# Two layers of a hybrid recurrent decoder on one core: another order of the projections' steps, and the norm's statistics shared between ScalarE and VectorE

## What is computed

```python
for l in range(DEPTH):                       # 2 layers; x is (tokens, 1024)
    x = sublayer(x, 0, lambda h: _swiglu(h, wg0, wu0, wd0))
    x = sublayer(x, 1, mixers)               # p = h @ w_in; 3 head groups; y @ w_out
    x = sublayer(x, 2, lambda h: _swiglu(h, wg1, wu1, wd1))

def sublayer(x, i, f):                       # shift, scale, gate = c @ w_ada + b_ada
    y = f(x * (1 + scale[i]) + shift[i])
    return LN(ALPHA * x + w[i] * (1 + gate[i]) * y)     # mean and variance over 1024 features

def mixers(h):
    p = h @ w_in                             # RWKV-7 part | GLA part | mLSTM part
    kk = k * k_k; kk = kk * rsqrt(sum(kk * kk, per head))   # RWKV-7: "KK"
    ...                                      # chunked recurrences of the three groups
    return concat(y_rwkv, y_gla, y_mlstm) @ w_out
```

## Time and profile before

| | us |
|---|---|
| median of three runs | 1681.7 |
| lowest and highest of them | 1667.69, 1681.84 |
| the profiled execution | 1677.3 |
| span of its profile | 1675.5 |
| busy: PE, DVE, ACT, POOL | 1608.5, 936.3, 667.0, 203.6 |

### The profile page before, as it was taken

One profiled execution on the slowest core, in us unless ns is written; L12 is line 12 of the kernel. 1 busy time (PEld: TensorE's weight loads), 2 busy tenths in 40 slices (PEclk: granted clock), 3 DMA queues, 4 the chain that ended last, 5 costly groups with the idle time before them and its releaser, 6 DMA issues. The chain is left out here.

```text
span 1675.5 us, 32875 instructions
## 1 busy us (share of the span) xinstructions
PE 1608.5 (96%) x14052; PEld 1480.5 (88%) x14052; DVE 936.3 (56%) x1605; ACT 667.0 (40%) x985; POOL 203.6 (12%) x271
## 2 busy tenths in 40 slices
PE   5999999999999999999999999999999999999997
PEld 2999998998767789999989999989877768899996
DVE  1544545586653775555474544466946456655544
ACT  2333334563323355333364333355532334543333
POOL 1000011100222330000110000210022242100011
PEclk9999999999997799999999999999989669999998
DMA  8765555533443174444755545654412116444441
GB/s 310 279 225 209 171 204 204 176 116 100 139 146 104 62 261 143 148 150 151 254 212 198 192 145 173 233 173 138 124 35 84 54 39 244 148 148 148 151 152 68
DMA packets 103864, 268.57 MB, mean 160 GB/s; under 512 B 39560, under 2 KB 42024, under 8 KB 103464
## 3 DMA queue, kind: packets, MB, share of 16 engines
q1 hardware_dynamic: 99304, 263.86, 46.3%
q10 hardware_dynamic: 4416, 2.62, 0.6%
HBM read 260.19 MB, written 6.26 MB: 159 GB/s over the span
## 5 line engine op out<-in xcount | busy, mean ns | idle before, releaser
L2410 DVE TENSOR_TENSOR wlo<-raw,whi 128x1024 fp32r<-128x1024 f32 x300 | 367.6, 1229 | 323.2 <-ACT whi L2261 320.9
L2261 ACT ACTIVATE whi<-raw 128x1024 fp32r<-128x1024 f32 x300 | 316.2, 1055 | 295.3 <-PE psV L2073 262.2
L2071 PE MATMUL psA<-XH,whi 128*128 128x320 f32 x1104 | 345.0, 313 | 7.9 <-DVE wlo L2410 7.5
L2073 PE MATMUL psA<-XH,wlo 128*128 128x320 f32 x1104 | 342.7, 310 | 0.0
L2072 PE MATMUL psA<-XL,whi 128*128 128x320 f32 x1104 | 342.6, 310 | 0.0
L2071 PE MATMUL psV<-XH,whi 128*128 128x320 f32 x848 | 267.1, 315 | 0.2
L2072 PE MATMUL psV<-XL,whi 128*128 128x320 f32 x848 | 263.8, 311 | 0.0
L2073 PE MATMUL psV<-XH,wlo 128*128 128x320 f32 x848 | 263.7, 311 | 0.0
L2071 PEld LDWEIGHTS psA<-XH,whi 128*128 128x128 f32 x1104 | 208.8, 189 | 10.8 <-issue 9.5
L2072 PEld LDWEIGHTS psA<-XL,whi 128*128 128x128 f32 x1104 | 208.7, 189 | 0.3
L2073 PEld LDWEIGHTS psA<-XH,wlo 128*128 128x128 f32 x1104 | 208.7, 189 | 0.0
(11 more groups left out here) (413 smaller groups left out, 2012.1 us busy)
## 6 DMA issues: line engine op xcount, KB each, us to landing
raw<-weights_dram SPq DMA_DIRECT2D x400, 512.0 KB, 3.4
own<-weights_dram SPq DMA_DIRECT2D x56, 512.0 KB, 5.9
in_xh<-weights_dram SPq DMA_DIRECT2D x6, 512.0 KB, 4.2
in_xl<-weights_dram SPq DMA_DIRECT2D x6, 512.0 KB, 5.0
raw<-weights_dram SPq DMA_DIRECT2D x6, 384.0 KB, 3.6
raw<-weights_dram SPq DMA_DIRECT2D x8, 256.0 KB, 3.8
in_hl<-weights_dram SPq DMA_DIRECT2D x4, 512.0 KB, 5.4
ZS<-st_rw_dram SPq DMA_DIRECT2D x2, 768.0 KB, 4.4
```

The costliest lines, as they stand in the source:

```text
L2071: mm(out, split_hi(n)[:, k], hi[:, kt], start=first, stop=False)
L2073: return mm(out, split_lo(n)[:, k], hi[:, kt], start=False, stop=last)
L2261: activation(split_hi(n), buffer(DENSE[n]), ACT.Copy).then_inc(hi_done, 1)
L2410: tt(split_lo(n), buffer(DENSE[n]), split_hi(n).bitcast(F32), ALU.subtract).then_inc(lo_done, 1)
```

## The change

Two parts. In the plan, the spreading of the RWKV steps over the projections 11 to 30 by a table of weights (RW_PRE, RW_TWICE, CV_AT) is replaced by a list written out (PROJ_MIXED). In the norm, ScalarE makes the square of the mean and the copy of the mean straight from PE's bank; the table load goes from the norm to the start of the product; the `MR` copy goes behind the inverse root; and VectorE's last split of the stage goes ahead of its arithmetic on the mean and variance. Three semaphores are new: `mean_full` (PE to ScalarE), `mean_squared` and `mean_kept` (ScalarE to VectorE, and the latter to PE, which may then use the bank again).

```diff
-RW_PRE = (2, 2, 2, 2, 3, 3, 2, 2, 2)
-RW_TWICE = (3, 5, 7)
-CV_AT = (4, 9, 12, 15, 18)
+PROJ_MIXED = ("rw 23 24 rw 25 26 rw cv 11 12 rw 13 rv 14 cv 15 rw 16 17 cv 27 rw 28 rv 19 cv 20 rw 21 cv 22 rw 29 rv 30 rw").split()
...
-    rest = [("proj", L, t) for t in PROJ_ORDER[NRW:]]
-    for k in CV_AT:
-        rest.insert(k, ("cv", L))
     out += after([("proj", L, t) for t in PROJ_ORDER[:NRW]], left)
-    out += spread([slot for k, w in enumerate(RW_PRE)
-                   for slot in ([(("rw", L), 1), (("rv", L), w - 1)] if k in RW_TWICE else [(("rw", L), w)])], rest)
+    out += [("proj", L, int(name)) if name.isdigit() else (name, L) for name in PROJ_MIXED]
...
-                        bV.close()
+                        bV.close(freed=None if means else (sem("mean_kept"), s + 1))
                         means.append(bank)
+                    mean_bank[s] = means[0]
...
-                    mm(means[0][:, 0:TOK], con("mean1024", P), ZT[:, DT - 1], start=False, stop=True).then_inc(sem("bankV_full"), 1)
+                    mm(means[0][:, 0:TOK], con("mean1024", P), ZT[:, DT - 1], start=False, stop=True).then_inc(sem("mean_full"), 1)
...
                 def product(n0, kts, s):
+                    nc.scalar.preload_act_table_set("natural_log_exp_and_others")
                     for d in range(DT):
...
                 def norm(s):
-                    nc.scalar.preload_act_table_set("natural_log_exp_and_others")
+                    act.wait_ge(sem("mean_full"), s + 1)
+                    A.do(activation(VR[:], mean_bank[s][:, 0:TOK], ACT.Square), sem("mean_squared"))
+                    A.do(activation(MN[:], mean_bank[s][:, 0:TOK], ACT.Copy), sem("mean_kept"))
+                    act.wait_ge(sem("var_ready"), s + 1)
+                    rsqrt(A, VR[:], sem("sd_ready"))
                     if s in THREE:
                         rows(*THREE[s])
-                    act.wait_ge(sem("var_ready"), s + 1)
-                    rsqrt(A, VR[:], sem("sd_ready"))
                     modulate(s + 1 if s < 3 * DEPTH - 1 else None, s)
...
                 def norm(s):
+                    split_to(n_next + LOCK - 1)
+                    fV.skip()
                     bank = fV.take()
-                    V.do(nc.vector.tensor_copy(MN[:], bank[:, 0:TOK]), sem("bankV_free"))
-                    V.settle()
-                    V.do(tt(VR[:], MN[:], MN[:], ALU.mult))
-                    V.settle()
-                    bank = fV.take()
+                    vec.wait_ge(sem("mean_squared"), s + 1)
                     V.do(tt(VR[:], bank[:, 0:TOK], VR[:], ALU.subtract), sem("bankV_free"))
                     V.settle()
                     V.do(ts(VR[:], VR[:], 0.0, LN_EPS / ALPHA ** 2, ALU.max, ALU.add), sem("var_ready"))
+                    vec.wait_ge(sem("mean_kept"), s + 1)
                     V.do(tt(ZT[:, 0], ZT[:, 0], MN[:], ALU.subtract))
-
-                    split_to(n_next + LOCK - 1)
```

More of the change, by code:

```diff
@@ L661, in hybrid_trunk @@
         half_bank, proj_bank = {}, {}
-        var_bank = {}
+        var_bank, mean_bank = {}, {}
         low_bank = {}
```

## The result

The changed kernel takes 1664.69 us in the median of 14 runs (1659.17 to 1675.89), the one before 1677.9 (14 runs, 1667.69 to 1684.95). The ratio is 0.9932, with a 95% interval from 0.9908 to 0.9956: 11.4 us less (7.4 to 15.4); the two medians stand 13.2 apart. The sum of the prediction was 10.4. The gain is clear of noise, and smaller than the one per cent (16.8 us) that the prediction took as the bound of a measurable change.

A forecast was written before the change was run, and what follows sets the result against it. PE was taken as the bound, busy 1608.5 of 1675.5 us. Projections -7.0 and norms -3.4 sum to -10.4, bringing the profiled 1677.3 to 1666.9; the median, 4.4 above, was put at 1671, range 1655 to 1682.

The forecast's parts named there:

- Part 1: New order of the projections: PE reaches the transposes L789 3.5 us earlier per layer, -7.0 us for two layers.
- part 2: New norm, ScalarE taking square and copy of the mean: PE gains over the six norms, -3.4 us in sum.
- B: Rival: PE's wait only moves to projection 29 or 30, some 2.5 us with half clock; 1678 us, chance 0.18.
- E: Rival: the norms give VectorE's full 1.27 us each, -7.6 for -3.4; 1667 us, chance 0.15.
- The place: Start of projection 22: PE idles for VectorE's low split, then runs at lower clock; 4.6 us a layer.
- (a): VectorE's splits of 22, 29 and 30 go ahead of the state steps; 4.6 us gained if nothing comes instead.
- (b): VectorE's new wait for ScalarE's later root of the KK sums: 4.6 us in all, bounds 0 and 7.0.
- (c): L778, sums over BB, moves behind projection 30, directly ahead of L789, uncovered: 1.0 us new PE idle time a layer.
- check by terms: Cross-check of the projections' -3.5 us a layer: -4.6 + 0.6 + 1.0, and some 0.5 for time per projection.
- case C: Rival, slower: root holds VectorE 7.0 us, PE waits 2.9 at 30, clock stays low in mixers; 1690 us, chance 0.07.

The follow-up runs named there:

- e3: Kernel before with only two RWKV steps moved, behind the splits of projections 20 and 21, old norm; ratio to before 0.9958.
- e4: Changed kernel with its projection order replaced by the one of e3, new norm kept; ratio to before 0.9937.
- e8: Kernel before once more, its order written out as a list, every engine's row the same; single run, projections 117.69 / 122.05 us.
- e5: Kernel before, old norm, with the changed order up to projection 28 and the order of before from there; ratio to before 1.0109.
- e7: Changed kernel with the table load moved back to the head of the norm; single run, six norms 50.47 us.
- e6: Changed kernel with a second table load ahead of the first in the out products; single run, 33.21 and 33.55 us from XH's end to the mean.
- e1: Kernel before with the new projection order alone, norm as before; ratio to before 0.9951.

## Why the prediction was right

- **The sum.** Part 1 was put at -7.0 and gave -6.6 in the profiled pair, part 2 at -3.4 and gave -3.9; that the total is met to 0.1 us (-10.5 for -10.4) is luck. The median was put at 1671 and is 1664.69: 3.8 of the difference lie in the start, since the median of three runs, 1681.7, is 1677.9 over 14. Neither B (a wait of 2 us or more at 29 or 30) nor E (norms 7.6 shorter) came.
- **The place.** 3.0 us of idle time and 1.6 for the clock in each layer. Without any wait the projections take 114.9 us (e3, e4), 4.4 less than before: right in sum. The 1.6 is no constant: e8 paid nothing in one layer.
- **(a) and (b).** VectorE's new wait was put at 1.7 + 2.9; it is 1.49 + 2.96. The split for 30 was put at 403.3; it ends at 403.2, in an execution that started layer 1's projections 0.6 us earlier and lost 0.68 in an early wait. What rested on this, that the work left behind the split pays for the new wait, is shown by e5, which has the wait without the move and is slower. PE's wait at 30 was put at 0.6; it is 0.2.
- **(c).** The idle time behind L778 was put at 1.0; it is 0.64 in both layers, and e3, which leaves L778 covered, has none. L789 was put at 409.4 and stands at 409.36; with the earlier start and the early wait just named, a part of this match is chance. The prediction's check by terms does not close as it stands: -4.6 + 0.6 + 1.0 is -3.0, and its own rows give 0.24 (two times 3.64 - 3.52) for the "some 0.5" that is to make it -3.5. The stretch gives -2.96 and -3.61 for -3.5.
- **The norms.** -0.6, -0.3, -0.6, -1.3, 0, -0.5 was the sum of 3.4; measured -0.85, +0.08, -0.87, -1.54, -0.24, -0.51, which is 3.93. That PE's gain is set by the gap chunks and not by VectorE's 1.27 is what e7 shows: 0.9 us more on VectorE moves PE in no norm but the last.
- **What was wrong.** Against case C stood that the mixers do not feel the clock, since both layers took equally long with different shares of it. The ten profiles show otherwise, as below. Case C did not come for another reason: there was no long wait to lower the clock. The sum had no term for early waits for a transfer, which some executions have.

Such a wait is the one in layer 1 of the changed kernel (ScalarE's split, then PE):

```profile
313.85 1.06 ACT L2256 ACTIVATE whi<-raw 128x1024 fp32r<-128x1024 f32 x1 [5.29 <-DMA raw<-weights_dram]
...
316.32 0.38 PE L2065 MATMUL psA<-XH,whi 128*128 128x320 f32 x1 [0.68 <-DVE wlo L2408]
```

ScalarE stands 5.29 us for a transfer, and PE 0.68 for the low split behind it. It is not the price of the faster norm: e4 and e6 have that norm and no such wait, e1 and e8 have the old one and waits of 0.93 and 1.09. Before and e8, whose rows are the same, have none and 1.09. It comes and goes with the execution; what makes a transfer late is open.

## What to carry to other kernels

Where an engine's queue is full, what it does first decides: find the one piece of work that the bottleneck waits for, and move only what stands directly ahead of it. Moving more than that can open idle time on the queue itself, which comes out at the bottleneck in full unless as much work has left its way (e5 against the changed kernel). A latency that fitted in its engine's idle time was free here (one load of 1.28 us in 1.40). One that does not fit can pass its first use without a wait and still cost about its excess further on, by way of what waits behind it in other engines' rows and queues (e6: 1.2 us at the split, 1.0 at the end of the product).

## What the hardware showed that was not expected

A large difference between the profiles lies in a stretch whose matmuls are in the same order in all ten kernels: the first layer's mixers take from 191.97 to 205.18 us, and 38.4 to 65.7 us of that are at half clock. A straight line through the ten points of the table has a slope of 0.41 us for each us at half clock. Here is where the changed kernel lost it, 15 us from the same matmul on; the changed kernel first, then before (windows):

```profile
core 0: us, PE busy (x) PEld busy (x) DVE busy (x) ACT busy (x) POOL busy (x), PEclk, DMA share, GB/s
545.48:560.48 15.00, 15.00 (x197) 12.73 (x199) 9.15 (x13) 3.06 (x5) 5.12 (x3) 0.50 0.01 2
```

```profile
547.97:562.97 15.00, 14.13 (x255) 10.84 (x257) 12.05 (x18) 4.48 (x7) 7.71 (x5) 0.70 0.01 4
```

PE is busy 15.00 of 15 us at 0.50 in the one, and gets through some 58 matmuls more in the other, at 0.70. Cut at the same matmuls, the whole stretch shows where the 5.24 us come from:

| layer 1's mixers, from matmul to matmul (line in before) | before: us, PEclk | after: us, PEclk |
|---|---|---|
| L789 to the matmul of `Tn`, L810 | 31.98, 1.00 | 33.03, 0.95 |
| on to that of `FOLD`, L2101 | 96.89, 0.86 | 96.92, 0.86 |
| on to that of `N`, L914 | 31.29, 0.67 | 35.43, 0.57 |
| on to the mean | 37.97, 1.00 | 37.99, 1.00 |

Where the clock is the same, the same matmuls take the same time; the two kernels come apart only where it is lower in one. So the mixers' 5.24 us are time at the lower clock, and no work that the change added. In layer 2 the stretch differs by less (193.76 to 197.82), as does its time at half clock (66 to 71 us), too little to read a slope from. What places the half clock in an execution stays open. The runs of one kernel differ with it too: over the 35 runs of before that were taken beside e1 to e4 (1664.09 to 1685.46 us) the mean clock lies between 0.949 and 0.968, and a straight line of the time against the time at half clock (twice 1 - clock, times the span) leaves 30% of the variance.
